# RMS norms whose sums of squares stand with tokens as rows, and whose factors are spread back by products with the identity

## The chip, the cores and the metric

The kernel runs on one core of one Trainium2 chip. The metric is the device time of one execution in microseconds, the median of several. All traces here are of one profiled execution.

## The reference

Two network blocks run one after the other in fp32 on 512 tokens of 1024 features. The first has four kinds of attention heads, a per-group norm, an output projection, a cross attention into 256 memory tokens and a squared-ReLU MLP. The second has two layers over 512 latent tokens, with 256 context tokens beside them in the first layer: attention, a gating branch, a convolution branch, and a gated convolution feed-forward. What the change touches is the norm ahead of nearly every projection:

```
def rmsnorm(x, g):
    y = x * lax.rsqrt(jnp.mean(x * x, axis=-1, keepdims=True) + 1e-6)
    return y * g
```

`norm_group` does the same within four groups of 256 features each (`y * rsqrt(mean(y*y))` per group).

## The kernel before, in words

Activations lie with features on the 128 partitions and tokens along the free dimension: `x` is 8 tiles (k = 0 to 7) of 128x512, the context `xc` and the memory `memx` 8 tiles of 128x256. Every projection is a `Gemm` or `GemmTok`: the weights come in slabs of 128x1024 (SyncE issues the DMA, a ring of five), GpSimd splits each slab into a high part `whi` and a rest `wlo` (L2329, L2331), and TensorE makes three products per block of 128 features (L305 to L307, or L395 to L397), 24 per output tile. An epilogue on ScalarE or VectorE takes the tile one step later.

The order is one list for all engines: it holds (part, step) pairs, and TensorE, ScalarE and VectorE each walk through the same list (`block.tensor`, `block.scalar`, `block.vector` at the end of the kernel) and issue what the part has for them at that step, strictly in order, with semaphores between them. `weave` puts the steps of one stage's parts between those of another's (context work between latent work); `then_norm` puts step k of a norm behind tile k of the projection that makes its input.

A `Norm` (L870) with K = 8 tiles runs over 18 steps. Steps 0 to 7: ScalarE squares tile k into one of two buffers (`tA`/`tB`, or `cA`/`cB` for the context, L910); TensorE multiplies it with a 128x128 stationary operand whose elements are all 1/1024 (1/256 in `norm_group`; `spread(self.mean)`, a column of the constants repeated) and adds up over k in one PSUM bank, which so holds the mean square of each token in every one of the 128 rows (L900). Step 8: ScalarE takes the root of the whole bank in place (L914, 128x512 or 128x256), VectorE the reciprocal in place (L930). TensorE has nothing at step 8 and goes on with the next part in the list. Steps 9 to 16: VectorE multiplies tile k by the gain and by the bank (L942), ScalarE rounds it to the high part `hhi` (L920, or with a shift L922), VectorE takes the rest `hlo` (L949 or L951), and the projection that follows waits for `hlo` tile by tile (`ready(k)`).

There are 13 norms. With 512 tokens: `norm_mix` at the start, `norm_group` (four banks, one per group, so four roots and four reciprocals), `norm_cross`, `norm_mlp`, `norm_final` (applies in place, no split), and `norm1` and `norm2` of both layers. With 256 tokens: `norm_mem`, and three of the context, `n1c`, `n2c`, `n1c1`. What stands beside step 8 in the list:

- `norm_mix`, `norm2` of layer 0, `norm1` and `norm2` of layer 1: nothing; the norm's own steps 9 to 17 follow.
- `norm_group`: steps 9 and 10, then `Branch` tiles (the last context branch `b_c`, an 8-block gate tile and an 8-block branch tile), then steps 11 on.
- `norm_mem`: step 9, then one `Branch` tile. `norm_cross`: steps 9 to 11, then `Branch` tiles. 
- `norm_mlp`: step 8 of `n2c` directly behind it, then the two norms' steps in turn.
- `n1c`: directly after its step 7, then a step of the softmax attention of the first block.
- `n1c1`: steps 7 to 12 in a row, then step 7 of `norm_final`, then its own steps 13 to 17, then step 8 of `norm_final`, then the first tile of `val_c1` (`GemmTok`, L395 to L397), whose input `n1c1` makes.
- `norm1` of layer 0: behind step 7, then a tile of `key_c1`, whose epilogue `QKHeads` has roots and reciprocals of its own (L574, L594).

Of the kernel before, what the change touches and what calls it, by code (L numbers as in the profile page):

```python
# [13 lines left out]
P = 128  # L14
# [74 lines left out]
def program(nc, rows, w, ada_in, x_in, xc_in, mem_in, cc_in, cols_in, cst_in, rel_in, onehot_in, toe_mask_in, lam_in,  # L89
            rope_in, tri_in, flip_in, sgu_in, out):  # L90
    with ExitStack() as ctx:
# [35 lines left out]
        small_d = [sb("small_d0", [P, 96]), sb("small_d1", [P, 96])]  # L127
        small_g = [sb("small_g0", [P, 64]), sb("small_g1", [P, 64])]
# [740 lines left out]

        class Norm(Part):  # L870
            def __init__(self, name, src, mean, hi, lo, gain, shift, stats, bufs, sq, ready, group=None, clear=()):
                self.src, self.mean, self.hi, self.lo, self.gain, self.shift = src, mean, hi, lo, gain, shift
                self.stats, self.bufs, self.sq, self.ready_x, self.clear = stats, bufs, sq, ready, clear
                self.name, self.K = name, len(src)
                self.group = group or [0] * self.K
                self.steps = 2 * self.K + 2 if hi is not None else 2 * self.K + 1

            def begin(self):
# [4 lines left out]
                self.rr, self.rr0 = take(name + "norm_recip", 1)  # L883
                self.app, self.app0 = take(name + "norm_applied", self.K)
# [7 lines left out]
            def tensor(self, pe, k):  # L892
                if k >= self.K:
                    return
                if k == 0:
                    for c in self.clear:
                        pe.wait_ge(*c())
                g = self.group[k]
                pe.wait_ge(self.q, self.q0 + k + 1)
                nc.tensor.matmul(self.stats[g], spread(self.mean), self.sq[k % 2], start=(k == self.group.index(g)),  # L900
                                 stop=(k == self.K - 1 or self.group[k + 1] != g)).then_inc(self.sum, 1)

            def scalar(self, act, i):
# [7 lines left out]
                elif i == K:  # L911
                    act.wait_ge(self.sum, self.sum0 + K)
                    for s in self.stats:
                        a = nc.scalar.activation(s, s, ACT.Sqrt, bias=cst[:, EPS_COL:EPS_COL + 1])  # L914
                    a.then_inc(self.rt, 1)
# [9 lines left out]
            def vector(self, dve, i):  # L925
                K = self.K
                if i == K:
                    dve.wait_ge(self.rt, self.rt0 + 1)
                    for s in self.stats:
                        v = nc.vector.reciprocal(s, s)  # L930
                    v.then_inc(self.rr, 1)
                    dve.wait_ge(self.rr, self.rr0 + 1)
# [1599 lines left out]
```

## Time and profile before

| | |
|---|---|
| median of 3 runs | 3927.58 us (3925.65 to 3928.03) |
| profiled execution | 3924.05 us, its span 3922.2 us, mean granted TensorE clock 0.956 |
| TensorE busy | 3605.9 us, 92% |
| VectorE busy | 1608.5 us, 41% |
| ScalarE busy | 968.2 us, 25% |
| GpSimd busy | 2022.7 us, 52% |

Busy time of TensorE (PE) is of matmuls; PEld is its loads of the stationary operand, which run beside them. An fp32 matmul leaves two records of each (two passes). In a row of the timeline the first number is the start in microseconds from the span's start, the second the time from the first start to the last end of the merged instructions, `x` their count, and the bracket the engine's idle time before them with what ended it.

### The profile page before, as it was taken

To read this page: it belongs to the slowest core of one execution; us is meant where nothing else is said; L and a number is where in the kernel's file an instruction comes from. 1 tells how busy PE (TensorE), PEld (TensorE's weight loads), DVE (VectorE), ACT (ScalarE), POOL (GpSimd) and SP (SyncE) were. 2 spreads that over 40 slices of the span, in tenths; PEclk is the share of its full clock that TensorE was granted. 3 is DMA by queue.
4 is the path that set the end of the run, shared out by engine and by line. 5 is a ranking of instruction groups with operands and counts; after the bars stand their busy time and mean duration, and the time that the engine had idled before them with its cause. 6 is when DMAs were issued, how large, how long until landed. Compare 5 with 4: busy or idle time off the path is not lost.

```text
span 3922.2 us, 46006 instructions
## 1 busy us (share of the span) xinstructions
PE 3605.9 (92%) x18218; PEld 2877.1 (73%) x18218; DVE 1608.5 (41%) x2741; ACT 968.2 (25%) x2040; POOL 2022.7 (52%) x1216
## 2 busy tenths in 40 slices
PE   7898779898899999899998899999999998999999
PEld 5776557676678988768776686887668766777887
DVE  6744432333863321564355313431372554214430
ACT  2134333322201211221244312220121343112210
POOL 4454225564457898745333264665544332455655
PEclk9999879999899999999999999999999999999999
DMA  6623113332564443332111122322322111222322
GB/s 227 230 93 104 46 38 99 113 107 70 197 203 132 138 141 127 115 118 76 65 53 45 54 91 75 97 91 82 117 70 76 54 54 44 74 88 80 97 84 100
DMA packets 109863, 389.18 MB, mean 99 GB/s; under 512 B 12057, under 2 KB 16537, under 8 KB 108242
## 3 DMA queue, kind: packets, MB, share of 16 engines
q1 hardware_dynamic: 89280, 315.10, 24.7%
q10 hardware_dynamic: 20370, 71.13, 5.3%
q8 instruction: 146, 2.39, 0.2%
q14 instruction: 67, 0.55, 0.0%
HBM read 379.86 MB, written 6.32 MB: 98 GB/s over the span
## 4 chain that ended last, share of the span: by engine, by line
PE 67%; DVE 8%; ACT 2%; issue 1%; POOL 1%; DMA 0%; DVEq 0%; ACTq 0%; SPq 0%
PE ps L305 19%; PE ps L307 18%; PE ps L306 18%; PE ps L1320 3%; PE ps L1332 1%; PE ps L395 1%; PE ps L900 1%; PE ps L396 1%; PE ps L397 1%; DVE ada L1784 1%; DVE junk L1784 1%; DVE small_d L1377 1%; PE ps L1300 1%; DVE ps L942 1%; PE ps L567 1%
## 5 line engine op out<-in xcount | busy, mean ns | idle before, releaser
L2329 POOL CAST whi<-raw 128x1024 fp32r<-128x1024 f32 (+1 forms) x606 | 618.1, 1020 | 1838.3 <-DMA raw<-in_w 1838.2
L2331 POOL TENSOR_TENSOR wlo<-raw,whi 128x1024 fp32r<-128x1024 f32 (+1 forms) x606 | 1416.9, 2338 | 48.5
L305 PE MATMUL ps<-hhi,whi 128*128 128x512 f32 x2056 | 853.5, 415 | 126.3 <-DVE hlo L951 23.7
L306 PE MATMUL ps<-hlo,whi 128*128 128x512 f32 x2056 | 828.1, 403 | 0.0
L307 PE MATMUL ps<-hhi,wlo 128*128 128x512 f32 x2056 | 827.3, 402 | 0.0
L305 PEld LDWEIGHTS ps<-hhi,whi 128*128 128x128 f32 x2056 | 395.4, 192 | 257.3 <-issue 45.9
L307 PEld LDWEIGHTS ps<-hhi,wlo 128*128 128x128 f32 x2056 | 395.7, 192 | 96.7
L306 PEld LDWEIGHTS ps<-hlo,whi 128*128 128x128 f32 x2056 | 396.7, 193 | 94.7 <-issue 6.7
L305 PE MATMUL ps<-chi,whi 128*128 128x256 f32 x864 | 259.3, 300 | 9.7 <-DVE mc_lo L867 3.9
L306 PE MATMUL ps<-clo,whi 128*128 128x256 f32 x864 | 248.6, 288 | 0.0
L307 PE MATMUL ps<-chi,wlo 128*128 128x256 f32 x864 | 247.9, 287 | 0.0
L1377 DVE TENSOR_REDUCE small_d<-ps 128x1 f32<-128x768 f32 x128 | 121.9, 952 | 203.3 <-PE ps L1320 203.3
L305 PEld LDWEIGHTS ps<-chi,whi 128*128 128x128 f32 x864 | 169.0, 196 | 20.8 <-issue 8.0
L594 DVE RECIPROCAL ps<-ps 128x512 f32<-128x512 f32 (+1 forms) x56 | 150.0, 2679 | 72.4 <-ACT ps L574 72.3
L621 DVE SCALAR_TENSOR_TENSOR f_sum<-ps,cols,f_sum 128x511 f32<-128x511 f32 x88 | 66.0, 750 | 261.9 <-ACT f_sum L666 261.9
L395 PE MATMUL ps<-whi,hhi 128*128 128x256 f32 (+1 forms) x512 | 149.5, 292 | 24.2 <-DVE ab_lo L1740 14.2
L306 PEld LDWEIGHTS ps<-clo,whi 128*128 128x128 f32 x864 | 169.0, 196 | 3.6 <-issue 2.4
L307 PEld LDWEIGHTS ps<-chi,wlo 128*128 128x128 f32 x864 | 168.9, 195 | 0.0
L1360 ACT ACTIVATE diff_p<-ps 128x512 f32<-128x512 f32 (+1 forms) x128 | 62.2, 486 | 380.7 <-PE ps L1300 380.7
L492 DVE SCALAR_TENSOR_TENSOR x<-ps,mod,x 128x512 f32<-128x512 f32 x32 | 24.0, 751 | 315.4 <-PE ps L307 315.4
L396 PE MATMUL ps<-wlo,hhi 128*128 128x256 f32 (+1 forms) x512 | 147.6, 288 | 0.0
L397 PE MATMUL ps<-whi,hlo 128*128 128x256 f32 (+1 forms) x512 | 147.2, 287 | 0.0
(368 smaller groups left out, 6398.1 us busy)
## 6 DMA issues: line engine op xcount, KB each, us to landing
raw<-in_w SPq DMA_DIRECT2D x574, 512.0 KB, 3.5
ada<-in_ada ACTq DMA_DIRECT2D x96, 512.0 KB, 3.9
raw<-in_w SPq DMA_DIRECT2D x16, 384.0 KB, 3.2
att_toe<-toe_dram ACTq DMA_DIRECT2D x12, 256.0 KB, 3.3
raw<-in_w SPq DMA_DIRECT2D x16, 192.0 KB, 2.3
x<-in_x SPq DMA_DIRECT2D x4, 512.0 KB, 9.8
cond<-in_cc ACTq DMA_DIRECT2D x2, 1024.0 KB, 4.9
kc_dram<-kc ACTq DMA_DIRECT2D x2, 1024.0 KB, 3.9
```

The lines of the kernel that those rows point to most:

```text
L305: nc.tensor.matmul(o, whi[:, buf, c], hi[:, k, 0:n], start=(k == 0), stop=False)
L306: nc.tensor.matmul(o, whi[:, buf, c], lo[:, k, 0:n], start=False, stop=False)
L307: mm = nc.tensor.matmul(o, wlo[:, buf, c], hi[:, k, 0:n], start=False, stop=(k == kt - 1))
L395: nc.tensor.matmul(o, self.hi[:, k, a], whi[:, s % RING, c], start=(k == 0), stop=False)
L396: nc.tensor.matmul(o, self.hi[:, k, a], wlo[:, s % RING, c], start=False, stop=False)
L397: mm = nc.tensor.matmul(o, self.lo[:, k, a], whi[:, s % RING, c], start=False, stop=(k == KT - 1))
L594: nc.vector.reciprocal(self.stats[m % 2], self.stats[m % 2]).then_inc(self.rr, 1)
L1320: mm = nc.tensor.matmul(pb(2 + 2 * a, n1 - n0, n0), self.q[r, h, b * P:(b + 1) * P], self.k[r, h, n0:n1], start=True, stop=True)
L1377: nc.vector.tensor_reduce(small[0][:, a:a + 1], pb(2 + 2 * a, TT), AX_X, ALU.max)\
L1784: nc.vector.tensor_tensor_reduce(self.ring[i % ADA_RING][:, :] if c else self.junk[:, :], self.ring[i % ADA_RING][:, :], ps[:, 1024 * (1 + ...
L2329: nc.gpsimd.tensor_copy(whi[:, buf, 0:c], raw[:, buf, 0:c]).then_inc(slab_hi, 1)
L2331: nc.gpsimd.tensor_tensor(wlo[:, buf, 0:c], raw[:, buf, 0:c], whi[:, buf, 0:c].bitcast(F32), ALU.subtract).then_inc(slab_split, 1)
```

## The change

The sums' products are turned round. The squared tile is now the stationary operand, one block of 128 tokens at a time, and the moving operand is one column of those constants: the mean square of 128 tokens comes out as one column with the tokens as rows. For 512 tokens that is four matmuls of one column per tile, for 256 two. `norm_group` has 16 columns, four for each group. At step 8 ScalarE takes the root of the 4, 16 or 2 columns from PSUM into a small SBUF buffer (`norm_factor`), VectorE the reciprocal in place. TensorE now has work at step 8: it waits for the reciprocal and spreads each column back over 128 partitions, with the column repeated 128 times as the stationary operand and the identity (128 columns) as the moving one, four matmuls per bank. VectorE waits for these before it goes on. Steps 9 to 17 are as before and read the same banks.

```diff
--- before.py
+++ after.py
@@ -125,6 +125,7 @@
         negsinks = sb("negsinks", [P, 4])
         small_s = sb("small_s", [P, 24])
         small_d = [sb("small_d0", [P, 96]), sb("small_d1", [P, 96])]
+        norm_factor = {"": sb("norm_f", [P, 16]), "c_": sb("norm_fc", [P, 8])}
         small_g = [sb("small_g0", [P, 64]), sb("small_g1", [P, 64])]
         Z = place_at[0]
         assert Z + 174 * KB <= nc.sbuf_usable_end, (Z, nc.sbuf_usable_end)
@@ -867,8 +868,11 @@
                 nc.vector.tensor_tensor(self.m_lo[:, m, :], o, self.m_hi[:, m, :].bitcast(F32), ALU.subtract).then_inc(tile_free[tile_bank[t]], 1)
 
 
+
         class Norm(Part):
             def __init__(self, name, src, mean, hi, lo, gain, shift, stats, bufs, sq, ready, group=None, clear=()):
+                self.n = stats[0].shape[-1]
+                self.factor = norm_factor[name]
                 self.src, self.mean, self.hi, self.lo, self.gain, self.shift = src, mean, hi, lo, gain, shift
                 self.stats, self.bufs, self.sq, self.ready_x, self.clear = stats, bufs, sq, ready, clear
                 self.name, self.K = name, len(src)
@@ -881,6 +885,7 @@
                 self.sum, self.sum0 = take(name + "norm_sum", self.K)
                 self.rt, self.rt0 = take(name + "norm_root", 1)
                 self.rr, self.rr0 = take(name + "norm_recip", 1)
+                self.sp, self.sp0 = take(name + "norm_spread", 1)
                 self.app, self.app0 = take(name + "norm_applied", self.K)
                 if self.hi is not None:
                     self.h, self.h0 = take(name + "norm_hi", self.K)
@@ -890,6 +895,15 @@
                 return (self.l, self.l0 + k + 1) if self.hi is not None else (self.app, self.app0 + k + 1)
 
             def tensor(self, pe, k):
+                blocks = [slice(j * P, (j + 1) * P) for j in range(self.n // P)]
+                if k == self.K:
+                    pe.wait_ge(self.rr, self.rr0 + 1)
+                    for g, o in enumerate(self.stats):
+                        for j, b in enumerate(blocks):
+                            c = len(blocks) * g + j
+                            mm = nc.tensor.matmul(o[:, b], self.factor[:, c:c + 1].to_broadcast([P, P]), ident,
+                                                  start=(j == 0), stop=True, skip_group_check=True)
+                    mm.then_inc(self.sp, 1)
                 if k >= self.K:
                     return
                 if k == 0:
@@ -897,8 +911,12 @@
                         pe.wait_ge(*c())
                 g = self.group[k]
                 pe.wait_ge(self.q, self.q0 + k + 1)
-                nc.tensor.matmul(self.stats[g], spread(self.mean), self.sq[k % 2], start=(k == self.group.index(g)),
-                                 stop=(k == self.K - 1 or self.group[k + 1] != g)).then_inc(self.sum, 1)
+                for j, b in enumerate(blocks):
+                    c = len(blocks) * g + j
+                    mm = nc.tensor.matmul(self.stats[0][:, c:c + 1], self.sq[k % 2][:, b], cst[:, self.mean:self.mean + 1],
+                                          start=(k == 0 and j == 0), stop=(k == self.K - 1 or self.group[k + 1] != g),
+                                          skip_group_check=True)
+                mm.then_inc(self.sum, 1)
 
             def scalar(self, act, i):
                 K = self.K
@@ -910,9 +928,9 @@
                     nc.scalar.activation(self.sq[i % 2], self.src[i], ACT.Square).then_inc(self.q, 1)
                 elif i == K:
                     act.wait_ge(self.sum, self.sum0 + K)
-                    for s in self.stats:
-                        a = nc.scalar.activation(s, s, ACT.Sqrt, bias=cst[:, EPS_COL:EPS_COL + 1])
-                    a.then_inc(self.rt, 1)
+                    c = len(self.stats) * self.n // P
+                    nc.scalar.activation(self.factor[:, 0:c], self.stats[0][:, 0:c], ACT.Sqrt,
+                                         bias=cst[:, EPS_COL:EPS_COL + 1]).then_inc(self.rt, 1)
                 elif i <= 2 * K and self.hi is not None:
                     k = i - K - 1
                     act.wait_ge(self.app, self.app0 + k + 1)
@@ -925,11 +943,10 @@
             def vector(self, dve, i):
                 K = self.K
                 if i == K:
+                    f = self.factor[:, 0:len(self.stats) * self.n // P]
                     dve.wait_ge(self.rt, self.rt0 + 1)
-                    for s in self.stats:
-                        v = nc.vector.reciprocal(s, s)
-                    v.then_inc(self.rr, 1)
-                    dve.wait_ge(self.rr, self.rr0 + 1)
+                    nc.vector.reciprocal(f, f).then_inc(self.rr, 1)
+                    dve.wait_ge(self.sp, self.sp0 + 1)
                 k = i - K - 1
                 if 0 <= k < K:
                     rstd = self.stats[self.group[k]]
```

## Rows read from the trace of the kernel before

**Rows 1.** The page: busy time, and the chain that ended last by engine.
```profile
PE 3605.9 (92%) x18218; PEld 2877.1 (73%) x18218; DVE 1608.5 (41%) x2741; ACT 968.2 (25%) x2040; POOL 2022.7 (52%) x1216
...
PE 67%; DVE 8%; ACT 2%; issue 1%; POOL 1%; DMA 0%; DVEq 0%; ACTq 0%; SPq 0%
```

**Rows 2.** Timeline, layer 0's second norm: from the last square to the next projection.
```profile
2404.66 1.28 ACT L914 ACT_TABLE_LOAD   x1
2404.70 1.12 PE L900 MATMUL ps<-tB,cst 128*128 128x512 f32 x2 [0.65 <-ACT tB L910]
2405.96 0.66 ACT L914 ACTIVATE ps<-ps,cst 128x512 f32<-128x512 f32 x1
...
2406.65 3.37 DVE L930 RECIPROCAL ps<-ps 128x512 f32<-128x512 f32 x1 [2.67 <-ACT ps L914]
...
2410.06 1.41 DVE L942 SCALAR_TENSOR_TENSOR ps<-x,gg,ps 128x512 f32<-128x512 f32 x2
...
2412.46 0.77 PE L305 MATMUL ps<-hhi,whi 128*128 128x512 f32 x1 [6.64 <-DVE hlo L951]
```

**Rows 3.** Line L930 alone: count, shortest, median and longest in ns.
```profile
L930 DVE RECIPROCAL ps<-ps x16: 1766/3365/3367, 22.9 to 3538.8; 128x512 f32<-128x512 f32 x12, 128x256 f32<-128x256 f32 x4
```

**Rows 4.** Groups by line and shape, VectorE and ScalarE: count, busy us, mean ns.
```profile
L1472 DVE RECIPROCAL small_d<-small_d 128x4 f32<-128x4 f32 x4 | 0.7, 168 | 0.0
...
L1453 ACT ACTIVATE small_d<-small_d,cst 128x4 f32<-128x4 f32 x4 | 1.2, 298 | 0.0
```

**Rows 5.** Timeline, TensorE: 12 fp32 passes of 128 columns in attention.
```profile
2001.28 1.42 PEld L1332 LDWEIGHTS ps<-v,diff_p 128*128 128x128 f32 x12
2001.39 1.50 PE L1332 MATMUL ps<-v,diff_p 128*128 128x128 f32 x12
```

**Rows 6.** Timeline, TensorE: an fp32 product of two columns, and the load behind it.
```profile
73.22 0.29 PEld L1860 LDWEIGHTS ps<-lams,cst 1*128 1x128 f32 x2 [0.37 <-issue]
...
73.53 0.19 PEld L305 LDWEIGHTS ps<-hhi,whi 128*128 128x128 f32 x1
```

**Rows 7.** Timeline, TensorE: a sum between two projection tiles.
```profile
3528.74 1.02 PE L900 MATMUL ps<-tB,cst 128*128 128x512 f32 x2
...
3529.60 0.19 PEld L306 LDWEIGHTS ps<-m_lo,whi 128*128 128x128 f32 x1 [0.24 <-issue]
```

**Rows 8.** Timeline, `norm_group`: four roots, the first application, the next projection.
```profile
741.25 2.39 ACT L914 ACTIVATE ps<-ps,cst 128x512 f32<-128x512 f32 x4 [2.55 <-PE ps L900]
...
756.72 1.41 DVE L942 SCALAR_TENSOR_TENSOR group<-y,cols,ps 128x512 f32<-128x512 f32 x2
...
760.66 0.80 PE L305 MATMUL ps<-hhi,whi 128*128 128x512 f32 x1 [13.76 <-DVE mc_lo L867]
```

**Rows 9.** Timeline, `norm_mem` and `norm_cross`: root, and the projection behind `norm_cross`.
```profile
822.60 0.45 ACT L914 ACTIVATE ps<-ps,cst 128x256 f32<-128x256 f32 x1 [11.81 <-PE ps L900]
...
861.32 0.66 ACT L914 ACTIVATE ps<-ps,cst 128x512 f32<-128x512 f32 x1 [2.54 <-PE ps L900]
...
871.06 0.80 PE L305 MATMUL ps<-hhi,whi 128*128 128x512 f32 x1 [4.10 <-DVE mc_lo L867]
```

**Rows 10.** Timeline, `norm_mlp` with `n2c`: both roots, and the first application.
```profile
978.76 1.02 ACT L914 ACTIVATE ps<-ps,cst 128x512 f32<-128x512 f32 x2
...
984.66 0.76 DVE L942 SCALAR_TENSOR_TENSOR ps<-x,cols,ps 128x512 f32<-128x512 f32 x1
```

**Rows 11.** Timeline, `n1c`, then `norm_final` with the first tile of `val_c1`.
```profile
204.36 1.77 DVE L930 RECIPROCAL ps<-ps 128x256 f32<-128x256 f32 x1 [5.00 <-ACT ps L914]
...
1601.62 0.64 ACT L914 ACTIVATE ps<-ps,cst 128x512 f32<-128x512 f32 x1
...
1603.03 0.38 ACT L452 ACTIVATE vc<-ps 128x256 f32<-128x256 f32 x1 [0.77 <-PE ps L397]
```

**Rows 12.** Timeline, VectorE in layer 0's first norm, woven with `key_c1`.
```profile
1636.72 3.37 DVE L930 RECIPROCAL ps<-ps 128x512 f32<-128x512 f32 x1 [9.71 <-ACT ps L914]
1640.12 1.77 DVE L594 RECIPROCAL ps<-ps 128x256 f32<-128x256 f32 x1
```

## The prediction

> **What bounds the kernel now.** The page comes first: TensorE is busy 92% of the span and holds 67% of the chain that ended last, VectorE 8% [rows 1]. So VectorE and ScalarE time is worth nothing where TensorE has other work, and everything where TensorE waits for it. The next view is the timeline around the norms, since these are the places where all of TensorE's work hangs on one short serial piece. Layer 0's second norm shows it bare [rows 2]: the last square is done at 2404.65, the table load for the root ends at 2405.94, the root runs 0.66, the reciprocal 3.37, and the first application starts at 2410.06; TensorE's next product starts at 2412.46 after 6.64 idle. From the root's start to the first application are 4.10 us, 3.37 of them one reciprocal over 512 equal columns in every row. The source view of the reciprocal says how often: 16, of which 12 are 128x512 and 4 are 128x256 [rows 3]. Behind the first application the eight tiles come at VectorE's pace (two operations of some 0.75 us for each tile, against three products), so whatever is saved ahead of it moves the whole ramp forward; no product in the ramp stands in the way.
>
> **What the change costs on TensorE in the sums.** Before, a sum of 512 tokens is two passes of 512 columns. Between two projection tiles it takes from 3528.74 to 3529.60: the load for the projection's second product starts there, 0.86 us later, with the projection's first product already running behind it; I count 0.86 [rows 7]. After, it is four blocks by two passes, eight passes that each load 128 columns of a stationary operand and stream one. The trace has no such long row of one-column products, so I bound a pass. From below: the two-column fp32 product has its two loads within 0.29 us, and one load lasts 0.19 to its end (the row behind it), so the second starts some 0.11 after the first [rows 6]. From above: from its first load to the load of the next instruction, which waits for a semaphore too, are 0.31 us for two passes, 0.155 each [rows 6]. The nearest row of many passes is attention's: twelve fp32 passes with loads of the same size and 128 columns streamed take 1.61 us from first load to last end, of which about 0.28 is the tail of the last, so 0.111 a pass [rows 5]. There a load costs nothing beside the products, which are longer than one column; I take 0.11. Eight passes are 0.88, against 0.86: the 72 sums of 512 tokens cost 72 x 0.02 = 1.4 us more at most, and the 32 sums of 256 tokens (four passes, 0.44) nothing. The last sum of a norm isn't on the path at all: the root waits for its table load until 2405.94 anyway, and the sum's end comes 0.1 before it [rows 2].
>
> A rule that speaks against the change: where a row shows twelve passes 0.111 apart [rows 5], the Trainium skill, TensorE: Matmul & The Clock Gate, Part 3 (what overlaps and what doesn't), says that a load of the stationary operand runs beside products in flight only where it goes to another group of rows. All loads here go to the same rows. By that rule attention's passes would be a load plus a stream, about 0.22 each, and the trace shows half of it; so the rule doesn't hold for this form, and I give it weight only through the second rival below.
>
> **What it costs and saves at step 8.** The root of 4 columns: ScalarE's 128x4 root in the head norms takes 0.298, VectorE's 128x4 reciprocal 0.168 [rows 4]; for 16 columns I add 0.08 to the latter. Hand-overs are 0.03 from ScalarE to VectorE, 0.04 between VectorE's own, both from the layer norm, and I take 0.10 from VectorE to TensorE, which is the gap between the end of `hlo` and the projection's first load or product there [rows 2]. The spread of one bank is four matmuls of 128 columns, eight passes: 1.61 less four passes of 0.111 is 1.17; of four banks, 32 passes, 1.61 + 20 x 0.111 = 3.83; of 256 tokens, four passes, 0.72 [rows 5]. At the lower clock a pass of 128 columns would be twice as long, which makes the eight passes 0.9 longer; I don't expect it, since at the layer norms TensorE has just run a projection, and keep it for the range. So root's start to first application, in the profiled execution's own time:
>
> - 512 tokens: 0.30 + 0.03 + 0.17 + 0.10 + 1.17 + 0.04 = 1.81 against 4.10, saved 2.29.
> - 256 tokens: 0.30 + 0.03 + 0.17 + 0.10 + 0.72 + 0.04 = 1.36 against 0.45 + 0.03 + 1.77 + 0.03 = 2.28 [rows 3, 9], saved 0.92.
> - `norm_group`: 0.30 + 0.03 + 0.25 + 0.10 + 3.83 + 0.04 = 4.55 against 756.72 - 741.25 = 15.47 [rows 8], saved 10.92.
>
> **Place by place.** Four norms stand alone (the first, and the three in the layers): 4 x 2.29 = 9.2, all on the path.
>
> `norm_group`: 10.9. TensorE waited 13.76 us there, to 760.66; between the last sum, just ahead of the root at 741.25, and 760.66 - 13.76 = 746.90 it made two `Branch` tiles, 5.7 us, while VectorE took reciprocals [rows 8]. The new wait stands ahead of them. They now begin at about 741.25 + 4.5 = 745.8 and end at 751.5, and the projection, at 760.66 - 10.9 = 749.8 by VectorE, starts at 751.5. This delay of 1.7 is absorbed in the ramp, which VectorE paces: its last tile comes 10.9 earlier whatever TensorE does. The full 10.9 stands.
>
> `norm_cross`: the same picture on a smaller scale. TensorE idled 4.10 behind two `Branch` tiles [rows 9]; they start 1.7 later, the projection 2.3 earlier, and that just fits: 2.3. `norm_mem`: 0.9, with one tile of 2.8 us (half of 5.7) beside it, which fits too.
>
> `norm_mlp` with `n2c`: both roots, both reciprocals (3.37 + 1.77) stand ahead of the first application, 984.66 - 978.76 = 5.90 [rows 10]. Now VectorE waits for the first spread before it takes the second reciprocal, so the chains follow each other: 0.30 + 0.20 + 0.10 + 1.17, then 0.21 + 0.10 + 0.72 + 0.04 = 2.84. Saved 3.1.
>
> `n1c`: a loss. Its reciprocal (1.77) held VectorE only while TensorE made the next scores [rows 11]. Now TensorE waits for root and reciprocal (0.6) and spreads (0.5 to 0.9, the clock is low around there) before the scores, which attention waits for: 1.3 later for them, against 0.8 less on VectorE. I count -0.5.
>
> `n1c1` and `norm_final`: `n1c1` gains its 0.9, but step 8 of `norm_final` now stands in front of the first `val_c1` tile. ScalarE reaches that root at 1601.62 - 0.9, VectorE its reciprocal after the context's last rest, at about 1601.3; the spread ends near 1602.6, and the tile (24 products of 256 columns as in a `Branch` tile, 2.8 us), which before was through by 1603.0 because it trickled along with its input [rows 11], ends at 1605.4: 2.4 lost, in a stretch that TensorE then fills without a gap. `norm1` of layer 0 follows: TensorE loses 0.6 + 0.9 at its step 8, but VectorE is what this stretch waits for (a second reciprocal starts 0.03 behind the first [rows 12]), and it is free 2.3 earlier. I take the two together as -0.1; the ends are +2.3, if the tile's delay is absorbed, and -3.9, if TensorE's 1.5 counts and VectorE's 2.3 doesn't.
>
> **The sum.** 9.2 + 10.9 + 2.3 + 0.9 + 3.1 - 0.5 - 0.1 - 1.4 for the sums = 24.4 us. The profiled execution took 3924.05 us, 1.85 more than its span, and is 3.5 below the median shown; a cut of this kind comes off either alike: 3927.6 - 24.4 = 3903.2, and I say 3903.
>
> **Rivals.** First, the slower side: loads of the sums aren't hidden. One mechanism: a pass of one column ends before the next operand is in, and the switch costs on top of the load. At the upper bound of 0.155 a pass [rows 6] a sum of 512 tokens takes 1.24 instead of 0.86, and of 256 tokens 0.62 instead of 0.43: 72 x 0.38 + 32 x 0.19 = 33 us more, nearly all between projection tiles where TensorE is the bound. Against the 25.8 saved without the sums that is 3935. It tips to slower than before at a pass of 0.144 (25.8 over 704 passes). For it: only this row has so few columns. Against: the row's second half holds a semaphore wait, and its two loads are 0.11 apart. The skill's rule above would put a pass at a load and a column, between these two.
>
> Second, TensorE's new wait at step 8 in the woven places takes back what VectorE gives: the `Branch` tiles behind it aren't made good in the ramp. Then `norm_group` keeps 10.9 - 4.5, `norm_cross` and `norm_mem` nothing, `n1c1` to `norm1` lose 3.9: 24.4 - 4.5 - 3.2 - 3.8 = 13, so 3915. For it: TensorE is 92% busy. Against: 13.76 and 4.10 us of idle time right there.
>
> Third, the waits removed were covered by something else, weights above all: GpSimd splits the slabs and used the idle time to get ahead. If it binds behind each norm, less than 8 us is left, 3921. Against: GpSimd is at 52% [rows 1], and in the layer norm TensorE's wait ends with VectorE's `hlo`, not with GpSimd [rows 2].
>
> **Chances.** Forecast 0.68 (3897 to 3911 as its own range); sums not hidden 0.16; woven places lose 0.10; weights bind 0.06. Of the first rival 0.10 ends over 0.2% slower (7.9 us, what a measurement can tell from no change): its 3935 is nearly there, and the lower clock would stretch it. 0.05 of it and half of the last fall within 0.2%. Faster 0.82, same 0.08, slower 0.10. The range: from 3893, if the clock stays up behind the shorter waits and the `val_c1` delay is absorbed, to 3919, which holds the second rival and sums at 0.12 a pass.
>
> **What would show it.** Reciprocals at L930's place of 0.17 us, no longer 3.37; eight loads of a sum 0.11 apart, and a sum between projection tiles still 0.86 to 0.9 (wrong if 1.0 or more); root's start to first application 1.8 in the layer norms and 4.5 in `norm_group`; TensorE's idle time ahead of their projections 6.64 less 2.3 in all, now in two pieces; the first `val_c1` tile done 2 us later than now. The prediction is wrong if the layer norms save less than 1.5 each, or if projections with sums between them last longer.

## The result, and the profile after

The changed kernel takes 3885.05 us (median of 4, 3881.36 to 3892.22) against 3926.61 (3925.18 to 3928.03) beside it: a ratio of 0.9894, 95% interval 0.9881 to 0.9906. That is 41.6 us less; forecast were 24.4. All the same the forecast's reasons fell, and the experiments below show it: the norms in their new form save nothing that can be measured here, and the 42 us come from something that the change does besides. (Of all executions below one stands apart and is in no ratio: one of the ten of `e10_ring32` took 5318.85 us at a granted clock of 0.618.)

The page of the profiled execution (3892.22 us, span 3890.4), with busy times, TensorE's granted clock in tenths over 40 equal slices and the chain by engine, answers to [rows 1]:

```profile
PE 3605.2 (93%) x18826; PEld 2953.6 (76%) x18826; DVE 1566.2 (40%) x2738; ACT 961.9 (25%) x2037; POOL 2027.2 (52%) x1216
...
PEclk9989878999999999899999999999999999999999
...
PE 80%; DVE 12%; ACT 4%; issue 2%; DMA 2%; POOL 1%; ACTq 0%; DVEq 0%; SPq 0%
```

VectorE's reciprocals of 3.37 and 1.77 us are gone, and it is busy 42 us less. TensorE has 608 loads and products more, and is as busy as before. The timeline of layer 0's second norm, which answers to [rows 2]:

```profile
2398.31 1.28 ACT L932 ACT_TABLE_LOAD   x1
...
2398.34 1.05 PE L916 MATMUL ps<-cst,tB 128*128 128x1 f32 x8 [0.72 <-ACT tB L928]
2399.60 0.26 ACT L932 ACTIVATE norm_f<-ps,cst 128x4 f32<-128x4 f32 x1
2399.90 0.18 DVE L948 RECIPROCAL norm_f<-norm_f 128x4 f32<-128x4 f32 x1 [2.27 <-ACT norm_f L932]
...
2400.13 1.93 PE L904 MATMUL ps<-cst,norm_f 128*128 128x128 f32 x8 [0.74 <-DVE norm_f L948]
...
2402.10 1.41 DVE L959 SCALAR_TENSOR_TENSOR ps<-x,gg,ps 128x512 f32<-128x512 f32 x2 [2.03 <-PE ps L904]
```

Root, reciprocal and hand-overs are as forecast (2400.13 - 2399.60 = 0.53; forecast 0.60). The spread lasts 1.93 instead of 1.17, so that root to application is 2.50: 4.10 before, 1.81 forecast. The views by windows say why; columns are the stretch, its length, busy us of PE, PEld, DVE, ACT and POOL, the granted clock, and the DMA's share and rate. The first two rows are the changed kernel before and in that spread. The next two are around `norm_group`'s sums, the fifth lies in its spread, and the last in its ramp, the stretch in which its eight tiles are applied one by one:

```profile
2396.00:2400.00 4.00, 2.68 (x20) 2.38 (x18) 0.85 (x2) 2.17 (x3) 1.59 (x1) 1.00 0.41 131
2400.40:2402.10 1.70, 1.67 (x8) 1.37 (x7) 0.00 (x0) 0.00 (x0) 1.53 (x2) 0.50 0.00 0
...
734.90:738.00 3.10, 3.10 (x30) 3.10 (x29) 0.00 (x0) 1.47 (x3) 0.00 (x0) 1.00 0.95 399
738.00:744.80 6.80, 6.80 (x34) 6.80 (x34) 0.00 (x0) 3.24 (x5) 5.46 (x4) 0.50 0.57 233
...
748.40:751.60 3.20, 3.20 (x17) 3.20 (x17) 0.00 (x0) 0.00 (x0) 3.12 (x3) 0.50 0.04 15
765.40:772.00 6.60, 5.07 (x13) 3.71 (x14) 4.07 (x5) 3.26 (x6) 2.57 (x1) 0.50 0.01 2
```

```profile
747.27 0.27 ACT L932 ACTIVATE norm_f<-ps,cst 128x16 f32<-128x16 f32 x1 [4.55 <-PE ps L916]
...
747.88 5.46 PE L904 MATMUL ps<-cst,norm_f 128*128 128x128 f32 x32 [0.65 <-DVE norm_f L948]
753.39 0.75 DVE L959 SCALAR_TENSOR_TENSOR group<-y,cols,ps 128x512 f32<-128x512 f32 x1 [5.56 <-PE ps L904]
```

Root to application is 6.12 where 4.55 were forecast, and 5.46 of it is the spread (forecast 3.83).

That leaves the gain. It isn't at the norms: up to the first application of `norm_mlp`, with the largest saving (`norm_group`) behind it, the changed kernel is 0.1 us ahead. At 2410 it is 8 ahead, at the end 32, all by the two profiled executions. It gathers where nothing was changed, which the prediction had no step for. In 100 us of layer 0's feed-forward, with TensorE never idle, the kernel before makes 430 products and the changed one 439 (windows of TensorE alone, before, then after):

```profile
2500.00:2600.00 100.00, 100.00 (x430) 1.00 0.30 95
```

```profile
2500.00:2600.00 100.00, 100.00 (x439) 1.00 0.32 96
```

(Columns: stretch, length, busy us with the count of products, clock, DMA share, GB/s.) Over all 512-column projection products that follow one another, the mean distance from start to start is 233.3 ns before and 229.3 after; over the 256-column ones 117.8 and 116.4. With 8700 and 5100 of them that is 35 + 7 = 42 us. What could slow the same product down? The change also allocates two tensors, 96 bytes per partition, ahead of `Z`, the base of all zone tensors: `Z` moved from 50528 to 50624, while the weight ring stayed at 2176.

### The profile page after: what moved, and what is told of

Its sections match the earlier page's. It is cut to its first block, busy times and chain, and to the rows that moved or that the text cites. A ratio compares the mean times of both kernels' runs of the same rounds, so it can differ in the third digit from the quotient of the medians.

```text
span 3890.4 us, 47216 instructions
## 1 busy us (share of the span) xinstructions
PE 3605.2 (93%) x18826; PEld 2953.6 (76%) x18826; DVE 1566.2 (40%) x2738; ACT 961.9 (25%) x2037; POOL 2027.2 (52%) x1216
## 4 chain that ended last, share of the span: by engine, by line
PE 80%; DVE 12%; ACT 4%; issue 2%; DMA 2%; POOL 1%; ACTq 0%; DVEq 0%; SPq 0%
PE ps L306 20%; PE ps L308 20%; PE ps L307 20%; PE ps L1337 3%; PE ps L916 2%; DVE ada L1801 2%; DVE junk L1801 2%; PE ps L396 2%; PE ps L398 2%; PE ps L397 2%; PE ps L1349 1%; DVE ps L959 1%; DVE small_d L1394 1%; PE ps L1317 1%; PE ps L1051 1%
## 5 line engine op out<-in xcount | busy, mean ns | idle before, releaser
L306 PE MATMUL ps<-hhi,whi 128*128 128x512 f32 x2056 | 842.5, 410 | 91.6 <-DVE hlo L966 14.6
L307 PE MATMUL ps<-hlo,whi 128*128 128x512 f32 x2056 | 818.7, 398 | 0.0
```

The costliest lines, as they stand in the source:

```text
L306: nc.tensor.matmul(o, whi[:, buf, c], hi[:, k, 0:n], start=(k == 0), stop=False)
L307: nc.tensor.matmul(o, whi[:, buf, c], lo[:, k, 0:n], start=False, stop=False)
```

## Experiments

**First set: placement or norms.** The theory (placement): `Z` modulo 64 sets the products' distance. The rival: the norms did it.

`e1_pad96`, the kernel before with the two allocations and nothing else:

```
+        sb("unused_f", [P, 16])
+        sb("unused_fc", [P, 8])
         small_g = [...]
```

> The kernel before with two tensors that nothing uses (64 and 32 bytes per partition) allocated where the change allocates its two. All that differs is that Z, the base of the tensors that the products read, lies at 50624 (a multiple of 64 bytes) and not at 50528 (32 past one). Theory P (placement): the start-to-start distance of the 512-column products falls from 233 to 229 ns, that of the 256-column ones from 117.8 to 116.4 ns, and with some 8700 and 5100 of them the time falls by about 42 us, to 3885 (3880 to 3892). Rival N (the new norms are what saved the time, directly or because the products follow each other differently): 3927, within 0.2%, distances as before. Theory P also says that the old norms keep all that they cost before.

Measured: 3885.15 us (3877.14 to 3889.65), ratio 0.9891 (0.9875 to 0.9907), as theory P had it. These are the old norms, and they have the whole gain.

`e2_change_unshifted`, the change with its two tensors behind all others:

```
-        norm_factor = {"": sb("norm_f", [P, 16]), "c_": sb("norm_fc", [P, 8])}
+        norm_factor = {"": zone("norm_f", [P, 16], 174), "c_": zone("norm_fc", [P, 8], 174.0625)}
```

> The change entire, with its two new tensors placed behind all others, so that Z stays at 50528 as in the kernel before. Theory P: the products' distances stay at 233 and 117.8 ns, and the time is that of the norms alone: 3927 give or take 8, since up to 985 us the changed kernel had gained nothing on the old one. Rival N: the time is that of the changed kernel, about 3885. Forecast on record for the norms alone: 3903; a time near it would say that the norms did what was forecast and that only the placement was missing.

Measured: 3927.48 us, ratio 1.0007 (0.9998 to 1.0016). So the new norms by themselves save nothing that can be measured: the interval goes from 0.8 us less time to 6.3 us more.

`e3_pad32` and `e4_pad64`, 32 and 64 unused bytes in the same place:

```
+        sb("unused_f", [P, 8])       # e3; [P, 16] in e4
```

> The kernel before with 32 unused bytes: Z at 50560, a multiple of 64 and of 128 bytes. Theory P with 64 bytes as what counts: as with 96 bytes, about 3885, distance 229 ns. If a multiple of 128 were needed, this one would be faster than the 96-byte one (50624 is an odd multiple of 64... 50624 = 791 x 64) and not equal to it. Rival N: 3927.

> The kernel before with 64 unused bytes: Z at 50592, again 32 bytes past a multiple of 64. Theory P: no change, 3927, distance 233 ns. A rival by which any shift, or another gap between the weights and the activations, gives the time: about 3885 to 3915 here. Rival N: 3927 here too, so this run speaks only together with the other two.

Measured: `e3_pad32` 3884.35 us, ratio 0.9890 (0.9874 to 0.9907), and `e4_pad64` 3928.11 us, ratio 1.0000 (0.9991 to 1.0010). The first keeps the gain, the second hasn't it, so "any shift" is out. With 32 bytes the 512-column distance was 227.4 ns, but the 256-column one 119.8.

Whether `Z` itself counts or its distance from the ring, two more kernels tell. `e10_ring32` puts 32 unused bytes ahead of the ring, which moves both; `e13_both32` puts 32 ahead and 32 behind.

```
+        sb("unused0", [P, 8])        # e10 and e13
         ring = place_at[0]
...
+        sb("unused1", [P, 8])        # e13 only
         Z = place_at[0]
```

> The kernel before with 32 unused bytes ahead of the weight ring: the ring moves from 2176 (a multiple of 128) to 2208, Z from 50528 to 50560 (a multiple of 128), their distance stays what it was. If the offset of the activations alone counts (as in the kernel with 32 unused bytes behind the ring, 3884.4): about 3885, 512-column distance 227 to 229 ns. If it is the offset of the two against each other (weights being loaded while activations are streamed): 3927 and 233 ns. If each must lie on 64 bytes of its own: 3927 too, or worse, since the 256-column products that stream weights would then be slower than before's 117.

> The kernel before with 32 unused bytes ahead of the weight ring and 32 behind it: the ring at 2208 and Z at 50592, each 32 bytes past a multiple of 64, and a multiple of 128 apart. If the distance between the loaded weights and the streamed activations is what counts: 3885 (3880 to 3890), 512-column distance 227 ns and 256-column 119.8 ns, as with 32 unused bytes behind the ring alone (same distance modulo 128). If each must lie on a multiple of 64 bytes: 3927, 233 ns.

Measured: `e10_ring32` 3927.97 us, ratio 1.0002 (0.9993 to 1.0012), with `Z` on a multiple of 128; `e13_both32` 3882.02 us, ratio 0.9890 (0.9873 to 0.9906), with both 32 bytes past a multiple of 64. So it is the distance between the two, and not where either lies:

| kernel | ring | Z | (Z - ring) mod 128 | 512 columns, ns | 256 columns, ns | us |
|---|---|---|---|---|---|---|
| before | 2176 | 50528 | 96 | 233.3 | 117.8 | 3926.6 |
| e2 (the change) | 2176 | 50528 | 96 | 233.3 | 117.9 | 3927.5 |
| e10 | 2208 | 50560 | 96 | 233.3 | 117.8 | 3928.0 |
| e4 | 2176 | 50592 | 32 | 233.3 | 117.5 | 3928.1 |
| e1 | 2176 | 50624 | 64 | 228.9 | 116.5 | 3885.2 |
| after (the change) | 2176 | 50624 | 64 | 229.3 | 116.4 | 3885.1 |
| e3 | 2176 | 50560 | 0 | 227.4 | 119.8 | 3884.4 |
| e13 | 2208 | 50592 | 0 | 227.3 | 119.7 | 3882.0 |

(Four executions each, ten of e2, e4 and e10.) The same stretch of 100 us with `e3_pad32`, windows of TensorE:

```profile
2500.00:2600.00 100.00, 100.00 (x443) 1.00 0.31 95
```

**Second set: where did the norms' 24.4 us go?** From here all kernels have the changed kernel's placement, and are to be compared with 3885.2 (old norms) and 3885.1 (new). Each has four executions, and the intervals of the ratios are about 6 us to either side; so of two kernels less than some 9 us apart the times alone don't tell which is faster, and the traces have to. Theory C: the one-column sums let the clock fall, in the spread and behind it. Rival D: it falls because TensorE waits, whatever it does between the waits. `e5_wide` lets the sums stream 128 equal columns and leaves the rest:

```
-  mm = nc.tensor.matmul(self.stats[0][:, c:c + 1], self.sq[k % 2][:, b], cst[:, self.mean:self.mean + 1],
-                        start=(k == 0 and j == 0), ...
+  mm = nc.tensor.matmul(self.stats[g][:, b], self.sq[k % 2][:, b], spread(self.mean),
+                        start=(k == self.group.index(g) and j == 0), ...
...
+  m = self.n // P
+  for g, o in enumerate(self.stats):
+      ac = nc.scalar.activation(self.factor[:, m * g:m * g + m], o[:, 0:self.n:P], ACT.Sqrt, ...)
```

> The changed kernel with sums that stream 128 equal columns per pass, where it streams one; the root then reads every 128th column (norm_group: four roots, one for each bank). Same loads, same number of passes, same waits; all that differs is how long TensorE's products are. Theory C (the clock falls because a run of one-column products leaves TensorE nearly without work): behind the sums of norm_final in the compressed stream's MLP (about 1506 us) the clock no longer falls; the layer norms' spread takes 1.17 and root to application 1.8 to 1.9 (2.50 in the changed kernel); norm_group 4.6 to 5 (6.12), and the 3.4 us that came back behind it (766 to 777) stay saved; the first norm's sums take 0.9 a tile. In all some 10 to 14 us less than the changed kernel's 3885: 3873 (3868 to 3878). Rival D (the clock falls because TensorE waits, whatever the sums stream): 3885 give or take 3, the layer norms at 2.5 as before. Rival E (128 columns make the sums dearer where TensorE is the bound): up to 3895.

Measured: 3873.50 us (3866.87 to 3884.63), ratio 0.9860 (0.9843 to 0.9876): 11.6 less than with one column, as theory C had it, and the two intervals don't meet. The same norm in its timeline, and, by windows, its spread and the stretch of `norm_group`'s sums:

```profile
2386.63 1.16 PE L918 MATMUL ps<-cst,tB 128*128 128x128 f32 x8 [0.61 <-ACT tB L930]
2387.89 0.26 ACT L935 ACTIVATE norm_f<-ps,cst 128x4 f32<-128x4 f32 x1
2388.18 0.18 DVE L952 RECIPROCAL norm_f<-norm_f 128x4 f32<-128x4 f32 x1 [2.27 <-ACT norm_f L935]
...
2388.41 1.16 PE L906 MATMUL ps<-cst,norm_f 128*128 128x128 f32 x8 [0.63 <-DVE norm_f L952]
...
2389.61 1.41 DVE L963 SCALAR_TENSOR_TENSOR ps<-x,gg,ps 128x512 f32<-128x512 f32 x2 [1.25 <-PE ps L906]
```

```profile
2388.40:2389.60 1.20, 1.16 (x8) 0.97 (x8) 0.00 (x0) 0.00 (x0) 0.92 (x1) 1.00 0.00 0
...
734.90:740.20 5.30, 5.30 (x47) 5.18 (x46) 0.00 (x0) 2.36 (x3) 4.93 (x4) 1.00 0.68 237
```

Root to application is 1.72 (forecast 1.81), the spread 1.16 (forecast 1.17). Waits and number of passes are those of the changed kernel, so rival D falls at these places. At one other it fits: ahead of the first `val_c1` tile, where TensorE mostly waits, and through the tile's first half the clock is at 0.50 in the wide kernel too, and it was low there before the change. First the wide kernel, then the kernel before:

```profile
1583.00:1586.00 3.00, 0.56 (x3) 0.27 (x2) 2.88 (x7) 1.79 (x4) 0.00 (x0) 0.50 0.00 0
...
1588.00:1590.00 2.00, 2.00 (x12) 2.00 (x11) 1.09 (x2) 0.00 (x0) 0.00 (x0) 0.50 0.03 8
```

```profile
1596.00:1600.00 4.00, 2.93 (x7) 1.90 (x8) 3.89 (x6) 2.03 (x4) 1.64 (x1) 0.50 0.00 0
```

In `norm_group` root to application is 745.25 - 740.31 = 4.94 (forecast 4.55; it now has four roots). One expectation missed: what comes back behind `norm_group` was to stay saved, and it is 5.6 us now; the last experiments are about that.

Two hybrids with one-column sums test the sizes: `e6_group_only` has the new form in `norm_group` alone, `e8_hybrid` everywhere but in `norm_mix`, `norm_cross`, `n1c` and `norm_final` (in each, the old branch is kept beside the new one):

```
+                self.rows = group is not None      # e6
...
+        norm_mix.rows = False                      # e8, and three like it
```

> Only norm_group in the new form, all other norms in the old one; placement as in the changed kernel, so it is to be compared with the old norms at that placement (3885.2). The forecast on record gives this norm 10.9 us: 3874. Theory C gives what the traces show of it: root to application 6.1 instead of 15.5, sums about 1 later, less 3.4 that come back behind it since the clock is low for products that ran at the full clock before: about 3 us, 3882 (3879 to 3884). If it comes out at 3885, nothing of it lasts.

> The new form in norm_group, norm_mem, norm_mlp, n2c, n1c1 and the norms of the layers; the old one in norm_mix, norm_cross, n1c and norm_final, placement as in the changed kernel. If the losses lie where the two traces show them (norm_mix 1.9, the stage behind n1c 2.3 to 4, norm_cross 0.7 to 3.5, norm_final's sums in the MLP 2.3 to 3.5 and its step ahead of the first val_c1 tile some 5), taking them out gives 3885 - 13 = 3872 (3867 to 3878). Rival (the clock's low stretches only move from one place to another): 3881 to 3886.

Measured: `e6_group_only` 3878.84 us (3875.84 to 3881.05), ratio 0.9878 (0.9864 to 0.9893), and `e8_hybrid` 3876.87 us (3870.28 to 3878.97), ratio 0.9871 (0.9856 to 0.9886). By the medians `norm_group` alone is worth 6.3 us, twice what theory C gave it and little over half of the forecast, and the choice of norms 8.2 where 13 were expected. But both intervals overlap those of the kernels that they are compared with. In the trace of `e6_group_only`, against `e1_pad96`, `norm_group` starts 6.4 earlier and 3.6 of it is lost up to 777, so 2.7 stay, about what theory C said; the rest of that execution's lead arises where the two kernels are the same. So these two runs neither confirm nor upset the sizes.

`e9_wide_final_old`: the wide sums, with `norm_final` in the old form.

```
+        norm_final.rows = False
```

> The wide sums, with norm_final alone in the old form, so that no step of it stands on TensorE ahead of the first val_c1 tile. In the wide kernel's trace this stage lost 6.7 us at the val_c1 tiles and gained 1.2 at norm_final's application. If the wait ahead of the tile is what costs it, about 5.5 less than the wide kernel's 3873.5: 3868 (3864 to 3873), and the DVE eviction of the first val_c1 tile no longer jumps. Rival: TensorE fills the gap later anyway: 3873.5.

Measured: 3866.81 us (3863.23 to 3870.94), ratio 0.9849 (0.9834 to 0.9864): 6.7 less than with wide sums everywhere, where 5.5 were expected. The intervals of the two overlap, so the time alone doesn't show it, but the trace does: from the end of `n1c1`'s last `clo` to ScalarE's eviction of the first `val_c1` tile are 0.79 us in the kernel before, 6.39 in the changed one, 5.93 with wide sums and 1.47 here, and VectorE's evictions of the first tiles no longer jump. Step 8 of `norm_final` ahead of the tile is what cost it.

Last, the ramp of `norm_group`. In the wide kernel it took back 5.6 us of the 10.3 that were saved ahead of it. `e11_wide_held` holds GpSimd's 98th slab until the last `hlo` of `norm_group`; `e12_wide_final_old_held` does it on top of `e9`.

```
                 pool.wait_ge(raw_loaded[buf], 16 * (n // RING + 1))
+                if n == 97:
+                    pool.wait_ge(*norm_group.ready(7))
```

> The wide sums, and GpSimd holds its 98th slab (the first that it splits within norm_group's ramp) until that norm's last hlo is written. In the wide kernel's profile four of the eight lo operations, which read two SBUF operands, last 2.75, 1.39, 2.08 and 2.07 us instead of 0.69, while GpSimd's operations run. Theory G (they shut each other out): all eight at 0.69, the ramp 5.5 us shorter, and GpSimd has 10 us of idle time behind it to catch up: 3868 (3864 to 3872). Rival H (the slabs are needed in the ramp or right behind it): TensorE waits for GpSimd instead, 3873 or more. Rival I (the operations are longer for another reason): they stay long, 3873.

> Both together, as the version to beat: wide sums, norm_final in the old form, GpSimd's 98th slab held. If the two savings add: 3862.5 (3858 to 3868).

The operation in question, `hlo` of `norm_group`: count, shortest, median and longest in ns. First with the old norms at this placement (`e1_pad96`), then with wide sums, last with the slab held:

```profile
L951 DVE TENSOR_TENSOR hlo<-group,hhi x8: 684/684/693, 757.1 to 768.7; 128x512 fp32r<-128x512 f32 x8
```

```profile
L970 DVE TENSOR_TENSOR hlo<-group,hhi x8: 684/1066/2750, 746.7 to 763.8; 128x512 fp32r<-128x512 f32 x8
```

```profile
L970 DVE TENSOR_TENSOR hlo<-group,hhi x8: 684/686/2619, 750.2 to 763.7; 128x512 fp32r<-128x512 f32 x8
```

Theory G holds at its place: held, seven of eight take 0.69, and the stretch from the first application to the eviction behind the ramp is 3.7 us shorter (16.7 instead of 20.4; 5.5 were expected, but the first `hlo` still meets an earlier slab). GpSimd's own rows in the wide kernel fit, the last three stretched too (1.04 to 1.50, 2.4 to 2.69):

```profile
746.50 2.41 POOL L2352 TENSOR_TENSOR wlo<-raw,whi 128x1024 fp32r<-128x1024 f32 x1
751.58 1.04 POOL L2350 CAST whi<-raw 128x1024 fp32r<-128x1024 f32 x1 [2.68 <-DMA raw<-in_w]
752.70 2.69 POOL L2352 TENSOR_TENSOR wlo<-raw,whi 128x1024 fp32r<-128x1024 f32 x1
755.34 1.50 POOL L2350 CAST whi<-raw 128x1024 fp32r<-128x1024 f32 x1
756.92 2.68 POOL L2352 TENSOR_TENSOR wlo<-raw,whi 128x1024 fp32r<-128x1024 f32 x1
```

But the end doesn't show it: `e11` 3872.20 us (3870.89 to 3876.89), ratio 0.9862 (0.9845 to 0.9878), `e12` 3866.80 us (3862.50 to 3867.54), ratio 0.9847 (0.9832 to 0.9861); 1.3 and 0.0 less than without it. The 3.7 us aren't lost right behind the ramp: between the traces of `e5` and `e11` the same VectorE instructions keep their distance within 0.3 us from 765 to 885. Whether something later takes them back or they drown in the spread of four runs stays open. `e9` and `e12` beat the kernel before by 60 us and the changed one by 18.

That VectorE and GpSimd shut each other out is what the Trainium skill says in SBUF — State Buffer, section "SBUF: two separate sides": an operation of VectorE with two SBUF inputs and one of GpSimd that reads SBUF take turns on a shared pair of ports, for whole instructions. The trace agrees: 2.07 instead of 0.69 us, and `hlo` of the layer norms, which takes one input from PSUM, stays at 0.75 through their ramps. It isn't peculiar to `norm_group`: the context norms' `clo` has two SBUF inputs too, and behind `norm_mlp` the first of them takes 1.80 us with wide sums (`e5`) and 0.48 with the old norms (`e1_pad96`). First the wide kernel, then the other:

```profile
973.93 1.80 DVE L972 SCALAR_TENSOR_TENSOR clo<-cC,mod,chi 128x256 fp32r<-128x256 f32 x1
```

```profile
984.76 0.48 DVE L953 SCALAR_TENSOR_TENSOR clo<-cC,mod,chi 128x256 fp32r<-128x256 f32 x1
```

## Why the prediction was wrong, step by step

The right direction was luck: placement by itself gives 42 us, as much as the whole change, and the forecast's own subject gave none. The table compares the start of the same VectorE instruction in two traces (us later; negative is earlier). For a norm it has the step from the VectorE instruction ahead of the norm's first application to that application:

| place | forecast | change, old placement | change, new placement | wide sums |
|---|---|---|---|---|
| `norm_mix` | -2.3 | +1.7 | +1.9 | -2.4 |
| `norm_group` | -10.9 | -4.8 | -6.4 | -10.3 |
| the ramp behind it | 0 | +4.1 | +3.8 | +5.6 |
| `norm_mem` | -0.9 | -1.1 | -1.1 | -1.0 |
| `norm_cross` | -2.3 | +0.8 | +3.6 | -2.2 |
| `norm_mlp`, `n2c` | -3.1 | -2.5 | -1.8 | -3.1 |
| first `clo` behind them | 0 | +0.7 | 0 | +1.3 |
| context MLP, 1487 to 1520 | 0 | +3.1 | +1.7 | 0 |
| `norm_final` | not given | -1.2 | -1.2 | -1.2 |
| first two tiles of `val_c1` | +2.4 | +6.7 | +6.8 | +6.7 |
| `norm1`, layer 0 | -2.3 | -2.4 | -2.1 | -2.0 |
| `norm2`, layer 0 | -2.3 | -2.4 | -1.6 | -2.4 |
| `norm1`, layer 1 | -2.3 | -1.7 | -2.4 | -2.4 |
| `norm2`, layer 1 | -2.3 | -2.0 | -2.1 | -2.4 |

(Columns: forecast; e2 against before; after against e1; e5 against e1. Steps of up to 3 us elsewhere are left out: stretches with a low clock don't fall alike in two executions, so the columns don't add up to the difference in time, and one step of 1 to 2 us means little unless several pairs of traces show it.)

- **A term that was missing, and the reason that the time fell outside the forecast: placement.** The sum has terms for what the change adds to and takes from the engines, and none for the 96 bytes that it adds ahead of `Z`: placement was put at nothing, without a reason. Shown by e1 and e2: all 42 us.
- **The step that failed: "I don't expect it, since at the layer norms TensorE has just run a projection".** The clock did fall. At layer 0's second norm the spread took 1.93 and not 1.17, so 1.60 of 2.29 was saved. `norm_mix`'s sums stayed at 0.21 a pass throughout, 1.84 a tile, where before the fourth tile was at 1.02 already; there the last sum is what the root waits for, and this norm lost 1.8. At `norm_group` 4.5 of the 10.9 were missing: the root came 3.0 late behind its sums, and the spread took 1.6 more. Of the 3.8 us that came back behind it 1.8 are products at the low clock, and 2.1 are the long `hlo` operations of the last bullet but one. I looked for the price of the clock in the spread only, and took 0.11 from attention, where passes of 128 columns run at a granted clock of 1.00 [rows 5]. Shown by e5: same passes and waits, 128 columns, 11.6 us less, and then every norm of the table starts within 0.6 us of the forecast.
- **The sums' cost at the full clock was right.** From a sum's first load to the load for the projection's second product are 3493.98 - 3492.86 = 1.12 us in the changed kernel and 3529.60 - 3528.51 = 1.09 before; the first rival (0.38 more) is out. (It is also the rival that the prediction means where it gives a rule weight only through its "second".) The loads, after and before:

```profile
3492.86 1.09 PEld L916 LDWEIGHTS ps<-cst,tB 128*128 128x128 f32 x8
3493.87 0.19 PEld L306 LDWEIGHTS ps<-m_hi,whi 128*128 128x128 f32 x1
3493.98 0.19 PEld L307 LDWEIGHTS ps<-m_lo,whi 128*128 128x128 f32 x1
```

```profile
3528.51 0.42 PEld L900 LDWEIGHTS ps<-tB,cst 128*128 128x128 f32 x2
```

  But at some sums the clock drops behind them, for products that the change doesn't touch. The context MLP shows it, in the timeline and by windows:

```profile
1504.44 1.05 PE L916 MATMUL ps<-cst,tB 128*128 128x1 f32 x8 [0.88 <-ACT tB L928]
...
1505.68 0.28 PE L308 MATMUL ps<-chi,wlo 128*128 128x256 f32 x1
...
1506.66 0.41 PE L308 MATMUL ps<-chi,wlo 128*128 128x256 f32 x1
```

```profile
1504.20:1506.00 1.80, 1.56 (x13) 1.56 (x14) 1.17 (x3) 0.65 (x2) 1.72 (x3) 1.00 0.77 189
1506.00:1509.40 3.40, 3.40 (x18) 3.40 (x17) 0.00 (x0) 0.00 (x0) 3.32 (x3) 0.50 0.15 59
```

- **`norm_final` ahead of `val_c1`: right mechanism, size wrong.** From the end of `n1c1`'s last `clo` to the first tile's eviction were 0.8 us; the forecast made it 4.1 (a spread that ends 1.3 behind the `clo`, and a tile of 2.8), and it is 6.4. Both parts were priced at the full clock, and here it is low: the spread takes 2.08 and ends 2.2 behind the `clo`, and the tile takes 4.2, its first half at 0.21 a product. At layer 0's `norm1` 2.1 come back (forecast 2.3). TensorE stands idle ahead of the spread:

```profile
1596.66 0.17 DVE L948 RECIPROCAL norm_f<-norm_f 128x4 f32<-128x4 f32 x1
...
1596.88 2.08 PE L904 MATMUL ps<-cst,norm_f 128*128 128x128 f32 x8 [3.44 <-DVE norm_f L948]
...
1598.61 0.56 PE L396 MATMUL ps<-whi,chi 128*128 128x256 f32 x1
...
1603.13 0.39 ACT L453 ACTIVATE vc<-ps 128x256 f32<-128x256 f32 x1 [6.76 <-PE ps L398]
```

In the old form this tile trickled along with its input [rows 11]. e9 takes the jump away. The clock is low here with wide sums too, so e5 didn't mend this part.
- **"Its last tile comes 10.9 earlier whatever TensorE does", of `norm_group`: the start was nearly right with wide sums (10.3), the ramp wasn't.** VectorE's pace in the ramp was taken as fixed. With the old norms (`e1_pad96`) GpSimd had split its slabs during the 15 us of waiting, and was idle from 755.5 to 774.0, over the whole ramp; with the wait gone it splits beside it. My third rival had GpSimd bind through missing weights; it binds through VectorE's operations, 5.6 us of them in e5, and already 2.1 in the changed kernel (two `hlo` of 2.08 and one of 0.91).
- **Right:** root 0.26 and reciprocal 0.18 (forecast 0.30 and 0.17), `norm_mem`, `norm1` of layer 0, and the starts of the other norms once the clock is held. The small loss at `n1c` stands in no clear step.

The account of the 24.4: with the clock held (e5) and `norm_final` in the old form (e9) the new norms are worth 18.3 (3885.15 less 3866.81, and these intervals don't meet). Of that 11.6 is the step to e5, and 6.7 the step to e9, the second by medians alone. Without its 2.4 for `val_c1` the forecast would be 26.8, so 8.5 are missing still. In the trace of e9 against `e1_pad96` VectorE's long operations beside GpSimd take back 5.6 in `norm_group`'s ramp, 1.5 behind `norm_mlp` and 1.1 in `n1c1`'s ramp, 8.2 together. That this is the missing part is read off the traces and not shown: e12 took away 3.7 of it, and the time didn't move.

## What to carry to other kernels

A change that allocates also moves: compare the kernel before with the allocations alone, before a gain is put down to the code. Products of one column kept TensorE "busy" in this profile while its clock fell, so a price for short passes taken from long ones wasn't theirs; with 128 columns to stream the clock stayed up, at 1.16 instead of 1.05 us for eight passes. And a wait removed in front of a stretch brings other engines' work into it: ask who was using that wait.

## What the runs showed of the hardware

- Products that stream one tensor while the next operand is loaded from another follow one another at a pace that depends on the distance of the two in bytes: at the four distances tried (modulo 128), 233.3 ns for 512 columns at 32 or 96 (four kernels), 227.3 to 229.3 at 0 or 64 (four kernels), 1% of the whole time here. At 0 the 512-column products are quickest and the 256-column ones slowest (119.8); at 64 it is 229 and 116.5, and the whole time is the same within the spread (3882.0 and 3884.4 against 3885.1 and 3885.2). That the two reads get in each other's way is the likely reason, and only argued. The Trainium skill, TensorE: Matmul & The Clock Gate, Part 2 (what each phase of a matmul is for), says that the loads don't take read bandwidth from the running product, since both have ports of their own; by these runs something between them does depend on the addresses.
- At distance 64 the pace has two levels within one execution. The wide kernel's profiled one (3884.63 us, against 3866.87 to 3876.95 of its others) made only 430 products in the stretch from 2500 to 2600 (row below): from 2400 to about 2675 they follow one another at 233.3 ns, on either side at 229. About 60 of its 257 runs of 20 products do, some 5 us in all; 15 and 18 do in the changed kernel and in `e12`, at most two in the other kernels at this distance. At distance 0 none is slower than 229. What sets the level stays open. It is one reason not to lean on differences of a few us between these kernels.

```profile
2500.00:2600.00 100.00, 100.00 (x430) 1.00 0.31 92
```

- Eight passes of one column, back to back, have the pitch of eight of 128: 1.05 against 1.06 to 1.16 us at the full clock. What they differ in is the clock that follows. The rule of the Trainium skill that the prediction quotes (TensorE: Matmul & The Clock Gate, Part 3), by which such a load would not run beside products in flight, doesn't hold for them either: the pitch is 0.11 us, with a load of 0.19 from start to end in each.
